# Sixteen modulation vectors: weights times values summed on VectorE, partitions added on TensorE

## The reference, cut to what matters

```
silu_c, silu_ctx = silu(c), silu(c_ctx)                # 1024 values each
mod_lat = silu_c   @ w_ada[l] + b_ada[l]               # w_ada[l]: 1024 x 6144
mod_ctx = silu_ctx @ w_ada[l] + b_ada[l]
sh1, sc1, gt1, sh2, sc2, gt2 = split(mod_lat, 6)       # the same six for the context
h = rms_norm(x, g) * (1 + sc1) + sh1
x = x + gt1 * mixer(h);  x = x + gt2 * mlp(rms_norm(x, g2) * (1 + sc2) + sh2)
```

## Time and profile before

| | us |
|---|---|
| median of 3 runs | 2072.3 (2071.34 to 2072.55) |
| profiled execution, first to last instruction (its span) | 2069.1 |
| TensorE busy (PE) | 2019.2 |
| VectorE busy (DVE) | 1129.0 |
| ScalarE busy (ACT) | 907.3 |

### The profile page before, as it was taken

How to read it: one execution, slowest core, us unless ns; L and a number is a source line. 1 busy time by engine, 2 the same in 40 slices (tenths; PEclk the granted TensorE clock), 3 DMA queues, 4 the chain that set the end, 5 groups by cost and what they waited for, 6 DMA issues and landing times. The chain is left out here.

```text
span 2069.1 us, 31601 instructions
## 1 busy us (share of the span) xinstructions
PE 2019.2 (98%) x12906; PEld 1680.2 (81%) x12906; DVE 1129.0 (55%) x2233; ACT 907.3 (44%) x1632; POOL 58.3 (3%) x83
## 2 busy tenths in 40 slices
PE   5999999999999999999999999999999999999998
PEld 3888767779777777898789899997877678888877
DVE  5447663446433343476665776642465444445886
ACT  4346762335423131265664554443434332233685
POOL 1000000001000000000000000000000000001100
PEclk9999999999999999999999999999999999999999
DMA  8222015533344444443116554444211243222311
GB/s 306 97 92 98 16 49 197 193 132 123 143 183 191 175 163 164 174 172 118 51 63 250 216 187 176 180 167 177 102 45 59 82 173 133 92 96 98 123 62 42
DMA packets 47104, 277.15 MB, mean 134 GB/s; under 512 B 4464, under 2 KB 12784, under 8 KB 16880
## 3 DMA queue, kind: packets, MB, share of 16 engines
q1 hardware_dynamic: 42080, 266.94, 34.2%
q10 hardware_dynamic: 4736, 7.34, 1.0%
q0 software_dynamic: 144, 0.85, 0.1%
HBM read 273.01 MB, written 2.10 MB: 133 GB/s over the span
## 5 line engine op out<-in xcount | busy, mean ns | idle before, releaser
L582 PE MATMUL ps<-t 128*128 128x512 f32 (+1 forms) x2176 | 754.0, 346 | 4.3 <-DVE t L1816 3.3
L584 PE MATMUL ps<-t 128*128 128x512 f32 (+1 forms) x2176 | 747.1, 343 | 0.0
L583 PE MATMUL ps<-t 128*128 128x512 f32 (+1 forms) x2176 | 747.0, 343 | 0.0
L1816 DVE TENSOR_TENSOR t<-t 128x1024 fp32r<-128x1024 f32 (+2 forms) x372 | 416.7, 1161 | 259.5 <-ACT t L1223 258.6
L582 PEld LDWEIGHTS ps<-t 128*128 128x128 f32 x2176 | 410.9, 189 | 68.2 <-issue 8.6
L1223 ACT ACTIVATE t<-t 128x1024 fp32r<-128x1024 f32 (+2 forms) x378 | 359.7, 999 | 222.4 <-PE ps L584 154.1
L584 PEld LDWEIGHTS ps<-t 128*128 128x128 f32 x2176 | 410.9, 189 | 50.6
L583 PEld LDWEIGHTS ps<-t 128*128 128x128 f32 x2176 | 410.9, 189 | 49.8 <-issue 0.7
L1802 DVE TENSOR_TENSOR t<-t 128x512 f32<-128x512 f32 (+10 forms) x621 | 228.8, 389 | 203.4 <-ACT t L1323 73.0
L1323 ACT ACTIVATE t<-ps 128x512 f32<-128x512 f32 (+1 forms) x244 | 115.8, 493 | 345.2 <-PE ps L584 238.6
L1811 DVE SCALAR_TENSOR_TENSOR t<-ps,t 128x256 f32<-128x256 f32 (+2 forms) x176 | 83.1, 496 | 179.8 <-PE ps L584 159.2
(11 more groups left out here) (167 smaller groups left out, 2092.5 us busy)
## 6 DMA issues: line engine op xcount, KB each, us to landing
t<-in_panels SPq DMA_DIRECT2D x235, 1024.0 KB, 4.8
t<-in_panels SPq DMA_DIRECT2D x18, 512.0 KB, 3.6
t<-in_panels SPq DMA_DIRECT2D x8, 768.0 KB, 4.1
t<-in_window ACTq DMA_DIRECT2D x4, 768.0 KB, 4.2
t<-in_ctxT SPq DMA_DIRECT2D x1, 1024.0 KB, 12.1
t<-in_xT SPq DMA_DIRECT2D x1, 1024.0 KB, 14.3
t<-in_ctxT ACTq DMA_DIRECT2D x1, 1024.0 KB, 5.7
t<-in_xT ACTq DMA_DIRECT2D x1, 1024.0 KB, 7.4
```

Of the source, the lines that this page charges most:

```text
L582: e.matmul(o, hi[:, k, w], xh[:, c0:c1], start=k == 0, stop=False)
L583: e.matmul(o, hi[:, k, w], xl[:, c0:c1], start=False, stop=False)
L584: t = e.matmul(o, lo[:, k, w], xh[:, c0:c1], start=False, stop=k == p.nk - 1)
L1816: e.tensor_tensor(p.half(wlo[p.buf], a), p.half(raw[p.slot], a), p.half(whi[p.buf], a).bitcast(F32), ALU.subtract).then_inc(*up(ve, ("lo", ...
```

## The change

The first two vectors stay as they are. For the other sixteen, VectorE multiplies each 128 x 1024 chunk of a piece by the column of values that belongs to it (one value for each partition) and adds it to a running sum `parts_of[x]`, x = 0 for the latent values and x = 1 for the context values. TensorE no longer touches the pieces: after the fourth it adds the 128 partitions with a selector column (`pick`, 32 columns of which one is 1), four products of 256 columns for each x. Five vectors that are used for latent tokens alone are made for x = 0 alone. The order of the vectors and the list `AFTER` are new: one piece behind each of 64 panels, none at a turn. In the MLP `beside(p)` on VectorE moves ahead of its work on p's results.

```diff
-AFTER = ([key for key in (("gm", 0, 0), ("mo", 0, 0), ("gn", 0, 1), ("gm", 0, 2), ("mo", 0, 2), ("gn", 0, 3)) for _ in range(2)]
-         + [("wo", 0, 3)] * 2 + [key for key in MLP_PANELS[4:-3:2] for _ in range(2)] + MLP_PANELS[-2:-1] + MLP_PANELS[-1:] * 3
-         + [("no", 1, 3)] + [("wo", 1, 3)] * 3 + [(kind, a) for kind in ("mq", "mk") for a in (1, 1, 3, 3)]
-         + [("mo", a) for a in range(4) for _ in range(2)])
+VECTORS = [("b", 0, v) for v in range(6)] + [("b", 1, 2), ("b", 1, 0), ("b", 1, 3), ("b", 1, 1), ("b", 1, 4), ("s", 0, 0), ("s", 0, 1),
+                                             ("b", 1, 5), ("s", 0, 2), ("s", 1, 0), ("s", 1, 1), ("s", 1, 2)]
+LATENT_ONLY = [("b", 1, v) for v in range(2, 6)] + [("s", 1, 2)]
+ADA = [(*v, q) for v in VECTORS for q in range(4)]
+AFTER = ([(kind, 0, h) for h in range(4) for kind in ("gm", "gn", "no")] + [("wo", 0, a) for a in range(3)] + MLP_PANELS[2:31]
+         + [("gn", 1, h) for h in range(4)] + [(kind, a) for kind in ("mq", "mk") for a in range(4)] + [("mo", a) for a in range(8)])
+WITH = {key: AT_START + n for n, key in enumerate(AFTER)}
...
         items.append(Panel(key, (*w, k0, n0), nk, n, len(items)))
-        while key[0] != "ada" and late:
-            ada(late.pop(0))
-        for i in WITH.get(key, []):
-            if len(WITH[key]) > 1:
-                late.append(i)
-            else:
-                ada(i)
+        if key in WITH:
+            ada(WITH[key])
...
# TensorE
-            def used(p, first=4):
+            def used(p):
                 mark(pe, ("used", p.i))
-                for i in WITH.get(p.key, [])[:first]:
-                    ada(i)
+                if p.key in WITH:
+                    q = WITH[p.key] % 4
+                    if q == 0:
+                        rows_out()
+                    if q == 3:
+                        vector_sums(WITH[p.key] // 4)
...
+            def vector_sums(r):
+                key = ("ada", r)
+                o = bank(key, (7,))
+                e.wait_ge(*done(("parts", r)))
+                n = 1 if VECTORS[r] in LATENT_ONLY else 2
+                for x in range(n):
+                    for j in range(4):
+                        t = e.matmul(o[32 * j:32 * j + 32, 0:256], pick[:, x, :], parts_of[x][:, j * 256:j * 256 + 256],
+                                     start=x == 0, stop=x == n - 1)
+                t.then_inc(*up(pe, ("full", key)))
+                taken[0] = 4 * r + 4
...
# VectorE
             def beside(p):
-                for i in WITH.get(p.key, []):
-                    if i % 4 == 0:
-                        rows_out()
-                    taken[0] = i + 1
+                if p.key not in WITH:
+                    return
+                i = WITH[p.key]
+                a, r = at["ada", i], i // 4
+                kind, l, v, q = ADA[i]
+                if q == 1:
+                    rows_out()
+                e.wait_ge(*landed(a))
+                w = a.view(raw[a.slot])
+                if q == 0 and i > AT_START:
+                    e.wait_ge(*done(("full", ("ada", r - 1))))
+                for k in range(2):
+                    for x in range(1 if VECTORS[r] in LATENT_ONLY else 2):
+                        c = sc[kind][:, 2 * q + k, x:x + 1]
+                        if q or k:
+                            e.wait_ge(*done(("part", x)))
+                            stt(parts_of[x][:, :], w[:, k, :], c, parts_of[x][:, :], ALU.mult, ALU.add, ("part", x))
+                        else:
+                            ts(parts_of[x][:, :], w[:, k, :], c, None, ALU.mult, None, ("part", x))
+                mark(ve, ("used", a.i), ("parts", r))
+                taken[0] = i + 1
...
                 for a in range(3):
                     begin(at["wo", l, a])
+                    beside(at["wo", l, a])
...
                             continue
+                        beside(at[f"ff{kind}", l, 4 * g + a])
                         for j in range(2):
...
-                        beside(at[f"ff{kind}", l, 4 * g + a])
```

More of the change, by code:

```diff
@@ L141, in plan @@
 def plan():
-    items, late = [], []
+    items = []
     def panel(key, w, k0, nk, n0, n):
         items.append(Panel(key, (*w, k0, n0), nk, n, len(items)))
-        while key[0] != "ada" and late:
-            ada(late.pop(0))
-        for i in WITH.get(key, []):
-            if len(WITH[key]) > 1:
-                late.append(i)
-            else:
-                ada(i)
+        if key in WITH:
+            ada(WITH[key])
     def cols(key, w, k0, nk, n0, n1, first=0):
@@ L340, in program @@
         arow = [sb([128, 256]) for _ in range(2)]
+        parts_of = [sb([128, 1024]) for _ in range(2)]
+        pick = sb([128, 2, 32])
         rst = sb([128, T])
@@ L714, in rms, with turn @@
                 e.matmul(o[:, a:b], ones[:, :], utmp2[0][:, a:b], start=True, stop=True).then_inc(*up(pe, ("full", key)))
-            def turn(s, p, key, xs, parts, c0, amid=(0, 5), vectors=4):
+            def turn(s, p, key, xs, parts, c0, amid=(0, 5)):
                 rows_out()
@@ L726, in turn @@
                                     amid=(amid[1], lambda: rms(s, "c")) if x == "l" and len(parts) == 2 and j == amid[0] else None)
-                used(p, vectors)
+                used(p)
             def softmax(s, units, PT, beside=None):
@@ L934, in first_layer @@
                     used(p)
-                turn(s, at["wo", l, 3], ("wo", l), lambda k: (gYh[:, k, :], gYl[:, k, :]), parts, q0, vectors=2)
+                turn(s, at["wo", l, 3], ("wo", l), lambda k: (gYh[:, k, :], gYl[:, k, :]), parts, q0)
                 if last:
                     rms(s, "l")
-                    for i in WITH[("wo", 1, 3)][2:]:
-                        ada(i)
                     mark(pe, ("xa free", "s0", "c"))
@@ L1244, in beside @@
             def beside(p):
-                for i in WITH.get(p.key, []):
-                    ada_out(i)
+                if p.key in WITH:
+                    ada_out(WITH[p.key])
             def stat(s, k, parts, free=()):
@@ L2183, in first_layer @@
                      None if last else at["ff1", l, 1])
-                beside(at["wo", l, 3])
                 after = "s0" if last else "n1.1"
@@ L2197, in first_layer @@
                                  at["mq", 1] if last else at["ckv", 1, 1])
-                            beside(at["ff2", l, 15])
                             continue
+                        beside(at[f"ff{kind}", l, 4 * g + a])
                         for j in range(2):
@@ L2242, in lstm_layer @@
                 for a in range(4):
-                    begin(at["mq", max(a, 1)])
+                    if a:
+                        begin(at["mq", a])
                     beside(at["mq", a])
@@ L2460, in vector @@
             e.memset(power[:, :], -0.5).then_inc(*up(ve))
+            e.memset(pick[:, :, :], 0.0).then_inc(*up(ve))
+            own()
+            for x in range(2):
+                e.memset(pick[:, x, x:x + 1], 1.0).then_inc(*up(ve))
             e.memset(epst[:, :], EPS).then_inc(*up(ve, "ones"))
@@ L2577 @@
     arrays["zones"] = zones()
-    nc = _bacc.Bacc("TRN2", target_bir_lowering=False, num_devices=1)
+    nc = _bacc.Bacc("TRN2", target_bir_lowering=False, num_devices=1, dynamic_dma_scratch_size=2048)
     f32 = _mybir.dt.float32
```

3 lines of the change are left out of this document (removed).

## The result

The changed kernel takes 2125.0 us (median of 4 runs, 2123.5 to 2126.1), the kernel before 2071.8 us (median of 4 runs beside it). The ratio is 1.0259, with a 95% interval of 1.0244 to 1.0274: slower by 53 us. The forecast was 2099 with a range to 2122, so the sign was right and the size 26 us short.

The account below looks back on a forecast made before the run. TensorE's unbroken stream of products was taken as the bound. Stops of 60.4 less a saving of 40.0 gave +20.3, the clock +6.6: 2069.1 became a span of 2096.0, median 2099 us, range 2064 to 2122.

Parts of the forecast that it names:

- The saving on TensorE: 64 pieces taken off TensorE, 59.8 us, less 12.6 for 27 rounds of sums: net 47.2 us, 40.0 on the path.
- What VectorE gets: VectorE's multiply-adds of 1024 columns: 1.28 us each, 4.9 a piece for both x, busy time from 1129 to about 1385.
- Rival (d): A multiply-add of 1024 columns on VectorE costs 1.50 us, each two-column piece 1.2 longer: 2136 us; chance 0.04.
- The loop through the slot: Load, split and VectorE's piece take 13.2 us a turn against TensorE's 10.88 panel; stops and late loads total 60.4 us.
- the loads that come late: Loads arriving late elsewhere in layer 0, outside the stops listed by stage: 1.0 us.
- bare turns: Turns that lose the old TensorE pieces which filled waits there: 7.2 us of the 47.2 saved is lost.
- The clock: Half of twelve stops and turns followed by half-rate products, 13 us, half given back: +6.6, bounds 0 and 24.
- rival (c): TensorE's clock falls after every stop: 12 stretches losing about 3 us, two thirds staying, 24 for 6.6: 2117 us; chance 0.15.
- The sum: Whole kernel: 2069.1 + 20.3 + 6.6 = 2096.0 us for the span, median 3.2 above: 2099.
- (a): The cover holds: VectorE's pieces end ahead of the sums and the whole saving stays, 2032 us; chance 0.13.
- (b): TensorE's stops are half as long, from earlier loads or more start for later vectors: 2065 us, 2055 to 2080; chance 0.13.

Follow-up runs that it names:

- run 2: Changed kernel with idle products of ones added on TensorE ahead of its wait in the ten rounds where it stood still; 2108.0 us, ratio 1.0177.
- piece-first run: Changed kernel with VectorE's order turned round: it does the piece before the next panel's low part; 2052.9 us, ratio 0.9913.
- Run 4: Changed kernel's places for the pieces, but TensorE multiplies them as in the kernel before and VectorE sums nothing; 2118.9 us, ratio 1.0228.
- run 12: TensorE's pieces in the changed kernel's places, with four panel slots in place of three; 2091.6 us, ratio 1.009.
- run 9: Piece-first kernel with five pieces given back to TensorE at layer 0's two turns and vectors 13 and 14 exchanged; 2048.1 us, ratio 0.9887.
- run 13: As run 9, but VectorE reads the transposed row out of PSUM before layer 1's first `no` low part; 2043.9 us, ratio 0.9863.

## Why the prediction was right or wrong

**The saving on TensorE.** Right. I said some 12 us busy for the rounds, and their line shows 23.0, but that column counts each product to its modelled end, and ten of the rounds ran wholly or in part at half clock (1.39 to 1.94 us, most 1.85 or more, where the same eight products take 1.07 in run 2). By the distance from the product before to the one behind, less the 0.23 us that lie between two neighbours in any case, a pair of pieces added 1.95 us in the kernel before, a round for both x adds 1.09 in the piece-first run, and a round for one x 0.66. That is 62.4 - 12.0 - 3.3 = 47.1 us, where I had 47.2.

**What VectorE gets.** Right: 1280 ns for the multiply-add of 1024 columns that the trace of before did not have, 765 for the one-operand form (0.75), 4.87 for a piece (4.9), busy 1374 (1385). Rival (d) is out.

**The loop through the slot.** Right in place and in size. The run with one column, the one with four slots, and the one with the piece first each change a different member of the loop, and each removes most of the stops. Forecast and measured stops at the sums:

| | forecast | measured |
|---|---|---|
| output of attention, three vectors | 5.8, 4.8, 9.4 | 8.0, 5.0, 8.1 |
| MLP, vector 5 | 4.4 | 4.3 |
| vectors 6, 8, 10 | none | none |
| vectors 7, 9, 11 | 4.9, 4.6, 4.6 | 3.9, 3.3, 3.6 |
| vector 12, and its row at the turn | 5.9 and 3.1 | 5.1 and 2.6 |
| `mq`, `mk` | 4.4, 4.0 | 6.0, 3.6 |
| layer 1's `gn` | 3.5 | 4.2 (four stops) |

Together that is 59.4 us forecast and 57.7 measured. With the loads that come late and the bare turns the forecast was 60.4 + 7.2 = 67.6 us more of idle TensorE, and it is 71.9. The turn into the MLP cost more than the 1.6 I took (5.7 us of idle), and the turn into the mLSTM layer stopped TensorE for 2.5 us where I had nothing.

**The clock: the step that failed.** I took half of the twelve stops to be followed by a stretch at the lower level, and half of that to be given back: +6.6, with an upper bound of 24. TensorE was busy for 30.0 us more than 2019.2 - 47.2. Counted product against the same product of the kernel before, those that follow one another without a pause take 21.5 us longer in all inside the stretches of the two traces, and the ten sums behind a stop take 8.0 us longer to the next product than in run 2, where they ran at full clock: 29.5 us for the clock. After the start, the trace has 15 stretches at half clock, 92.2 us together, with TensorE busy for 68.9 of them; before it had one of 6.8. Every stop at a sum was followed by one. The windows behind the stops of vectors 2, 9 and 12 and of the turn into the mLSTM layer:

```profile
348.60:352.00 3.40, 3.36 (x20) 1.89 (x21) 0.00 (x0) 0.38 (x1) 0.00 (x0) 0.50 0.67 220
744.80:748.20 3.40, 3.40 (x20) 1.90 (x21) 1.66 (x4) 0.39 (x1) 0.00 (x0) 0.51 0.67 231
893.40:904.00 10.60, 8.04 (x54) 6.79 (x55) 5.68 (x12) 3.41 (x6) 0.00 (x0) 0.61 0.72 254
1427.40:1430.80 3.40, 3.40 (x9) 2.65 (x9) 3.40 (x4) 0.58 (x2) 0.00 (x0) 0.50 0.02 5
```

Both halves of the assumption were wrong. The stretches came behind all of the ten stops and not half of them, besides five at the turns and in layer 1; and little was given back. Run 2 takes the stretches of the ten stops away: of 22.5 us of faster products 18.0 are in its span, so a fifth was given back, not half. The other 5 to 7 us lie at the turns and in layer 1, which that run leaves alone; that is a difference and not a run. So rival (c) had the mechanism, and its size too: net of what was given back the clock cost about 25 us by these numbers, against its 24 and my 6.6.

The Trainium skill, in "TensorE: Matmul & The Clock Gate", section "HAM oscillation", says that waits between bursts of products drop the clock each time anew. This trace agrees for the ten stops at sums, of 3.29 to 8.14 us. I had the rule and one case in the trace that bore it out, and gave it 0.15 because short gaps, of about 1 us, left the clock alone. But the stops that I forecast were 3 to 9 us long, and no row of that length spoke against the rule. One spoke for it, which I had left out when I wrote of a single case: at the start of the kernel before, TensorE stands for 5.09 us from 32.7, and what follows runs at half clock.

```profile
32.70:37.80 5.10, 0.02 (x1) 0.05 (x1) 3.02 (x7) 2.88 (x5) 0.55 (x1) 0.56 0.96 377
37.80:43.50 5.70, 5.70 (x27) 5.70 (x28) 5.70 (x8) 4.71 (x9) 1.89 (x3) 0.50 0.53 217
```

The sum: 20.3 + 6.6 = 26.9 was forecast for the span and 54.7 is measured. With the clock at 29.5 in place of 6.6 and the idle time at 71.9 in place of 67.6 it is 54.1. The clock is 18 to 23 of the 28 us that were missing; the lower figure counts what was given back with the waits, which without the slow products would have been some 4.5 us longer.

**The other rivals.** (a) needed a piece of 2.8 us or less; with pieces of 2.6 the run with one column takes 2046.9, so the point from which it decides was right, though not the 2032 it was to give. (b) is out: the stops are as long as forecast.

**What the prediction did not see.** It spoke of the places of the pieces only as 7.2 us of lost cover. Run 4 prices the same places at 47 us with TensorE's pieces. So the change is not a method with a small cost of re-ordering: the re-ordering costs 47 where TensorE does the pieces, and the method there adds 6 with three slots and takes 31 with four. Of run 4's 47 us, 27 are slots by run 12. Of the other 20, run 12's trace shows 6.5 at the turns (TensorE stands 2.7 us longer at the one behind the MLP and 3.8 at that of layer 1) and 7.4 in that a piece alone adds 1.09 us and one of a pair 0.975; the clock is 0.3. The remaining 6 or so stay open.

## What to carry to other kernels

When work moves to an engine with room, ask first what that engine's piece holds while it waits in order, here a slot of three, and write down one full turn of the loop (load, copy, subtraction, piece) beside the time of a panel; a busy share of 36% doesn't show a loop that is longer than a panel. Put what frees a resource ahead of what waits for that resource: two calls exchanged were worth 72 us, more than the work that the change took off TensorE. And price each stop of several us of TensorE with the slow products behind it as well, until a row shows otherwise; here that was some 30 us on top of 72, of which a fifth came back where it could be tested.

## What was not expected of the hardware

- A stretch at half clock cost less than half its length: 92.2 us of them cost about 29.5, as TensorE was busy for only 68.9 of them; some begin within the stop itself or hold another.
- Idle products on TensorE during its stops, 49.2 us of them, made the whole kernel 17 us faster and left the busy time of VectorE (1374.5 us against 1374.1) and ScalarE (909.6 against 908.7) as it was.
- The clock did not fall at every pause. In the changed kernel the stop of 2.36 us at 327.1 left it at 1.00, and so did, in the piece-first run, this one of 2.96 us:

```profile
843.90:846.90 3.00, 0.05 (x4) 0.02 (x1) 1.89 (x4) 1.12 (x4) 0.00 (x0) 1.00 0.80 320
846.90:859.00 12.10, 12.09 (x100) 11.97 (x100) 5.02 (x10) 2.84 (x6) 0.00 (x0) 1.00 0.24 88
```

  while in the changed kernel one of 2.54 at the turn into the mLSTM layer was followed by 0.50 from 1427.4 on.
- Nor does a low clock need a long stop, or come each time. In layer 1's attention of run 9, pauses of 0.57 and 0.83 us stand at 967.3 and 970.4 and only shorter ones beside them (TensorE busy for 3.74 us of 5.60), and the clock is 0.50 behind them. In run 13 the same products with the same two pauses, 1.4 us later, are followed by 1.00. So 1.6 us of the difference between the two runs is chance, as far as these traces show. Run 9, then run 13:

```profile
966.00:971.60 5.60, 3.74 (x26) 2.30 (x25) 5.11 (x12) 4.07 (x10) 0.00 (x0) 1.00 0.01 3
971.60:975.00 3.40, 3.40 (x19) 3.17 (x17) 1.62 (x5) 1.66 (x4) 0.00 (x0) 0.50 0.86 308
...
968.00:973.00 5.00, 3.14 (x20) 1.71 (x19) 4.51 (x12) 3.96 (x9) 0.00 (x0) 1.00 0.02 3
973.00:977.00 4.00, 4.00 (x35) 3.76 (x34) 3.78 (x10) 3.32 (x8) 0.00 (x0) 1.00 0.69 262
```
